# Six ring slots instead of eight, two weight chunks kept in SBUF, and the expert product one slot behind the dot

## The chip, the cores and the metric

The kernel runs on one core of a Trainium2 chip. The metric is device time in microseconds (us) of one execution, as the median of several. An execution with the hardware profiler on gives the trace; its own time stands beside its span below.

## What is computed

Two decoder layers over 256 tokens of width 1024, in float32. Layer 0 mixes tokens with differential attention, layer 1 with a short gated convolution; each is followed by a PEER expert layer: every token picks 8 x 16 = 128 of 16384 single-neuron experts and needs the rows u and v of each. The part that fills the time is this:

```python
q = (xt @ w_q).reshape(T, PEER_HEADS, 2, PEER_HALF)
s = jnp.einsum('thpd,hpkd->thpk', q, sub_keys).astype(F32)
s_top, i_top = lax.top_k(s, PEER_TOPK)
...
best, pos = lax.top_k(cand, PEER_TOPK)
idx = jnp.take_along_axis(cand_idx, pos, axis=-1)
gates = jax.nn.softmax(best, axis=-1)
...
    act = jnp.einsum('chkd,cd->chk', u_tab[ib], xb)
    act = (jax.nn.gelu(act.astype(F32)) * gb).astype(xb.dtype)
    return jnp.einsum('chk,chkd->cd', act, v_tab[ib])
```

## The kernel before

**Windows and slots.** There are four windows: the two blocks of 128 tokens, in layer 0 (windows 0 and 1) and in layer 1 (windows 2 and 3). A window has 128 slots, 512 in all. In a slot each of the 128 tokens (one per partition) uses one of its experts. POOL gathers the 128 rows (u beside v, 8 KB each, 1.05 MB together) into a slot of `ring` with an indirect DMA (L643). DVE multiplies u with the token's row and sums (`dot`, L1239). ACT makes the gelu, the weight and a diagonal matrix of the weights (`weigh`, L853, L855, L859). PE multiplies this diagonal with v into two PSUM banks that add up over the window (`add_expert`, L575: two calls, four matmul records in the trace) and raises `v_used`. At a window's end DVE adds the banks to the residual (`finish`, L1231), and the next window's first product waits for that (`acc_read`).

**The ring.** `ring` has 8 slots. The gather of slot s waits for `v_used` of slot s - 8 (L640), so a slot is busy from the issue of its gather until its expert product is done. The first eight gathers wait instead for products of the front (everything that runs before slot 0), since the ring's memory first holds weight chunks.

**Weight chunks.** The other operations of the next window (projections, attention or convolution, output, queries and ranking) are woven into the slots of the present one. A chunk of a weight matrix is 2 MB and is used by 8 matmul calls, one in each of 8 slots (L338, `project`). Chunks live at numbered places: 0 and 1 are the two halves of `wring` and are used in turn, 2 to 5 are pairs of ring slots and serve only the front, 6 is `spare`. SP issues the loads in one list (`loads`, L259 to L268). A load waits until the product on the chunk that held its place is written, and all loads behind it in the list wait with it. Chunk ("wq", 3) of windows 2 and 3 is one matrix part: it is loaded once, into place 6, and read in both windows.

**The order of work.** Every engine runs a loop over the slots and, at slot s, does its expert step and then every side step that is due at s. The due times are a table of numbers (`AT`, and the `LATE_` tables). On DVE and ACT the expert step at slot s is that of slot s. On PE it is that of slot s - 2 (L585 to L590). The side steps pass data between engines: PE makes a product, ACT copies it, PE transposes, DVE reads, each one or two slots later. An engine that waits for such a datum also holds up its later expert steps.

Of the kernel before, what the change touches and what calls it, by code (L numbers as in the profile page):

```python
# [14 lines left out]
P = 128  # L15
D = 1024
# [9 lines left out]
NKEYS = 128  # L26
EXPERTS = NKEYS * NKEYS
SLOTS = PH * TOPK
RING = 8
WINDOWS = DEPTH * (SEQ // P)  # L30
ALL = WINDOWS * SLOTS
CHUNK = 512
# [80 lines left out]
def along(sides, slot):  # L113

    for side in sides:
        while side["due"] is not None and side["due"] <= slot:
            side["due"] = next(side["steps"], None)
# [6 lines left out]
def build(nc, consts, x_rows, x_cols, bias_rows, ffn_rows, w_qkv, w_o, conv_w_in, conv_w_out, peer_w_q, peer_keys, peer_uv, out):  # L124
    with ExitStack() as ctx:
        def sb(name, shape, dt=F32):
            return ctx.enter_context(nc.sbuf_tensor(name, shape, dt))
# [4 lines left out]
        def sem(name):  # L132
            return ctx.enter_context(nc.semaphore(name))
# [15 lines left out]
        qk_gain, sub_gain, taps = of_const("qk_gain"), of_const("sub_gain"), of_const("taps")  # L149
        lam4 = of_const("lam").rearrange("p (i d) -> p i d", i=4)  # L150

        ring = sb("ring", [P, RING, 2 * D])
        wring = sb("wring", [P, 2, KT * CHUNK])
        rows = sb("rows", [P, 3 * D])
        rows1 = sb("rows1", [P, 2 * D])
# [41 lines left out]
        gains = sb("gains", [P, 2])  # L197
        dots = sb("dots", [P, RING])
        gelu = sb("gelu", [P, RING])
        weight = sb("weight", [P, RING])  # L200
        diag = sb("diag", [P, RING, P])

# [3 lines left out]
        def pool_of(name, banks=None):  # L206
            return Pool(banks or [psum(f"{name}0"), psum(f"{name}1")], [sem(f"{name}_written{i}") for i in range(2)],
                        [sem(f"{name}_read{i}") for i in range(2)])

        pp, tt, ss, ff = pool_of("pp"), pool_of("tt"), pool_of("ss"), pool_of("ff", acc)  # L210
# [29 lines left out]
        xf_made = sem("xf_made")  # L240
        uv_in = [sem(f"uv_in{i}") for i in range(RING)]
        dot_done = sem("dot_done")
# [18 lines left out]
        loads = [(0, *what) for what in first]  # L261
        later = [(1, "in", 2), (1, "in", 1), (0, "wq", 2), (1, "in", 3), (0, "wq", 3)]
        for n in range(1, WINDOWS):
            later += [(n, "in", c) for c in (2, 4, 3, 5, 0, 1)] if n > 1 else []
            later += [(n, "out", 0), (n, "out", 1), (n, "wq", 0), (n, "wq", 1), (n, "wq", 2), (n, "wq", 3)]
        later = [what for what in later if what not in ((2, "wq", 3), (3, "wq", 3))]
        loads += [(*what, (i + 1) % 2) for i, what in enumerate(later)]
        loads.insert([load[:3] for load in loads].index((2, "wq", 0)), (2, "wq", 3, 6))  # L268
        held_at = {}
        for place in range(7):  # L270
            for i, load in enumerate(load for load in loads if load[3] == place):
# [2 lines left out]
        def ring_at(s):  # L274
            return (s + 4) % RING

        def slot(s):

            return ring[:, ring_at(s), :], uv_in[ring_at(s)], 16 * (s // RING + 1)
# [17 lines left out]
        def weights(n, what, c):  # L297

            if (n, what) == (1, "in") and c in (0, 4, 5):
                n = 0  # L300
            if (n, what, c) == (3, "wq", 3):
                n = 2
            place, before = held_at[(n, what, c)]
            return places[place], w_in[place], 16 * (before + 1)

        def copied(eng, pool, *keys):

            for key in keys:
                eng.wait_ge(pool.read_sem(key), pool.times(key) + 1)

        def written(eng, pool, key):

            eng.wait_ge(pool.written_sem(key), pool.times(key) + 1)
# [5 lines left out]
        def _(pe):  # L319
# [93 lines left out]
            def front():  # L413
                low, high, every = range(4), range(4, KT), range(KT)
                pe.wait_ge(const_in, 16)
                pe.wait_ge(x_scaled, 1)
                pe.wait_ge(w_half_in, 16)
                first, _, _ = weights(0, "in", 0)
                by_row = first.rearrange("p (k n) -> p k n", k=KT)
                bank = take(pp, (0, "in", 0))  # L420
# [143 lines left out]
            def add_expert(s):  # L564

                n, k = divmod(s, SLOTS)
                if s == 0:
                    copied(pe, ff, (1, "in", 4), (1, "in", 5))
                if n and k == 0:
                    pe.wait_ge(acc_read, n)  # L570
                row, landed, count = slot(s)
                pe.wait_ge(landed, count)
                pe.wait_ge(diag_ready, s + 1)
                for half in range(2):
                    mm = nc.tensor.matmul(acc[half][:, :], diag[:, s % RING, :], row[:, D + half * 512:D + (half + 1) * 512],  # L575
                                          start=(k == 0), stop=(k == SLOTS - 1))
                mm.then_inc(v_used, 1)
# [5 lines left out]
            for n in (2, 3):  # L583
                sides += begun(gated_input(n), turn_gated(n), output(n), turn_output(n), *(experts(n, c) for c in range(4)))
            for s in range(ALL):  # L585
                if s > 1:
                    add_expert(s - 2)
                along(sides, s)
            add_expert(ALL - 2)
            add_expert(ALL - 1)  # L590


        @block.sync
        def _(sp):
            def load(n, what, c):
                place, landed, _ = weights(n, what, c)
                matrix = {"in": in_dram[n // 2], "out": out_w_dram[n // 2], "wq": peer_w_q[n // 2]}[what]
                if (n, what, c) == (0, "in", 0):
                    half = KT * CHUNK // 2
                    sp.dma_start(place[:, 0:half], matrix[c][:, 0:half]).then_inc(w_half_in, 16)  # L600
                    sp.dma_start(place[:, half:], matrix[c][:, half:]).then_inc(landed, 16)
                else:
                    sp.dma_start(place, matrix[c]).then_inc(landed, 16)

            sp.dma_start(xT[:, :, :].rearrange("p k t -> p (k t)"), x_cols[0]).then_inc(x_cols_in[0], 16)
            previous = {}
            for n, what, c, place in loads:
                if place in previous:
                    m, was, k = previous[place]
                    written(sp, pp, (m, "wqb" if (m, was, k) == (0, "wq", 0) else was, k))  # L610
                if place == 6:
                    sp.wait_ge(logit_max, 4)
                    written(sp, pp, (1, "values", 1))
                previous[place] = n, what, c
                load(n, what, c)
            for b in range(2):
                for c in range(2):
                    sp.wait_ge(h_finished, 2 * (2 + b) + c + 1)
                    sp.dma_start(out_dram[b][:, c * CHUNK:(c + 1) * CHUNK], h[:, b, c * CHUNK:(c + 1) * CHUNK]).then_inc(out_done, 16)
            sp.wait_ge(out_done, 64)  # L620


        @block.gpsimd
        def _(pool):
            for n in range(WINDOWS):
                for k in range(SLOTS):
                    s = n * SLOTS + k
                    if k % TOPK == 0:
                        pool.wait_ge(idx_ready, s // TOPK + 1)
                    if s < RING:  # L630
                        if ring_at(s) < 2:
                            written(pool, ff, (1, "in", 4))
                        elif ring_at(s) < 4:
                            written(pool, ff, (1, "in", 5))
                        elif ring_at(s) < 6:
                            written(pool, ff, (1, "in", 0))
                        else:
                            written(pool, pp, (0, "out", 0))
                    else:
                        pool.wait_ge(v_used, s - RING + 1)  # L640
                    dst, landed, _ = slot(s)
                    at = s % (2 * SLOTS)
                    nc.gpsimd.indirect_dma_start(dst, None, uv_dram, bass.IndirectOffsetOnAxis(idx[:, at:at + 1], 0)).then_inc(landed, 16)  # L643
# [229 lines left out]
        def _(dve):  # L873
            done = [0]

            def link(ins):

                done[0] += 1
                ins.then_inc(dve_step, 1)
                dve.wait_ge(dve_step, done[0])  # L880
# [343 lines left out]
            def finish(n):  # L1224

                b = n % 2
                yield SLOTS * (n + 1) + 1
                dve.wait_ge(v_used, SLOTS * (n + 1))
                for c in range(2):
                    hh = h[:, b, c * CHUNK:(c + 1) * CHUNK]  # L1230
                    link(nc.vector.tensor_tensor(hh, hh, acc[c][:, :], ALU.add))  # L1231
                    dve.sem_inc(h_finished, 1)
                dve.sem_inc(acc_read, 1)

            def dot(s):
# [5 lines left out]

            front()
            sides = begun(*(finish(n) for n in range(WINDOWS - 1)))
            sides += begun(second_head(), late_input(2), late(1), late_input(1), attention(0), late(2), late_input(3), late(3), attention(1),
                           output(1), *(experts(1, c) for c in range(4)))
            for n in (2, 3):
                sides += begun(gated_input(n), convolve(n), output(n), *(experts(n, c) for c in range(4)))
            for s in range(ALL):
                dot(s)
                along(sides, s)  # L1250
            whole(finish(3))


# [46 lines left out]
```

## Time and profile before

| | us |
|---|---|
| median of 3 runs (1577.06 to 1578.72) | 1578.14 |
| the profiled execution's own time | 1575.86 |
| its span in the trace | 1574.0 |
| front, until the first gather is issued | 101.6 |
| PE busy in matmuls | 1357.4 (86%) |
| DVE busy | 1005.6 (64%) |
| moved by DMA | 637.58 MB, mean 405 GB/s |
| of it the gathers | 536.90 MB |

PE, DVE, ACT and POOL are the engines; SP only issues loads. Times within the trace count from the span's start. The busy time of an overlapped matmul record is longer than its share of the engine: four records of an expert product follow each other in 1.72 us though the line says 1.88. A name with a q (DVEq) is the engine's sequencer. The idle time in brackets is that of the engine before the instruction, with what ended it.

### The profile page before, as it was taken

To read this page: it belongs to the slowest core of one execution; us is meant where nothing else is said; L and a number is where in the kernel's file an instruction comes from. 1 tells how busy PE (TensorE), PEld (TensorE's weight loads), DVE (VectorE), ACT (ScalarE), POOL (GpSimd) and SP (SyncE) were. 2 spreads that over 40 slices of the span, in tenths; PEclk is the share of its full clock that TensorE was granted. 3 is DMA by queue.
4 is the path that set the end of the run, shared out by engine and by line. 5 is a ranking of instruction groups with operands and counts; after the bars stand their busy time and mean duration, and the time that the engine had idled before them with its cause. 6 is when DMAs were issued, how large, how long until landed. Compare 5 with 4: busy or idle time off the path is not lost.

```text
span 1574.0 us, 13058 instructions
## 1 busy us (share of the span) xinstructions
PE 1357.4 (86%) x3288; PEld 587.2 (37%) x3288; DVE 1005.6 (64%) x2442; ACT 594.8 (38%) x1809; POOL 568.2 (36%) x516
## 2 busy tenths in 40 slices
PE   7899899888897988977989898879898887777777
PEld 3454344433343433333434343334343332222222
DVE  5686879964587864444467985444558896544454
ACT  1324354543342542332334443333334444333333
POOL 0024333543343433323444343323344453444341
PEclk9999999999998999989999899999899999999999
DMA  9469999999999999999999999999999999999996
GB/s 399 208 250 422 423 417 407 407 422 421 422 422 421 394 422 423 425 421 422 422 422 422 389 410 423 423 422 422 422 422 421 420 407 421 421 421 422 421 422 282
DMA packets 82297, 637.58 MB, mean 405 GB/s; under 512 B 9136, under 2 KB 9264, under 8 KB 10544
## 3 DMA queue, kind: packets, MB, share of 16 engines
q0 software_dynamic: 73728, 536.90, 82.4%
q1 hardware_dynamic: 7200, 93.85, 14.3%
q10 hardware_dynamic: 1296, 6.00, 0.9%
q8 instruction: 28, 0.46, 0.1%
q14 instruction: 45, 0.37, 0.1%
HBM read 635.67 MB, written 1.05 MB: 405 GB/s over the span
## 4 chain that ended last, share of the span: by engine, by line
DMA 39%; PE 36%; DVE 16%; ACT 4%; issue 4%; DVEq 0%; POOL 0%; SPq 0%; POOLq 0%; ACTq 0%
DMA ring<-in_peer_uv_dram,idx 38%; PE acc L575 22%; PE pp L338 10%; DVE ring L1239 7%; PE acc L338 1%; ACT diag L859 1%; PE tt L351 1%; DVE top_i L1025 1%; ACT weight L855 1%; DVE top L1021 1%; ACT L853 1%; ACT L722 1%; DVE row_f L1070 1%; ACT gelu L853 1%; PE pp L425 1%
## 5 line engine op out<-in xcount | busy, mean ns | idle before, releaser
L575 PE MATMUL acc<-ring,diag 128*128 128x512 f32 x2048 | 1003.9, 618 | 160.4 <-ACT diag L859 150.9
L1239 DVE CUSTOM_DVE_ANT_0 ring<-ring,xf 128x1024 f32<-128x1024 f32 x512 | 626.9, 1226 | 492.2 <-DMA ring<-in_peer_uv_dram,idx 480.5
L643 POOL DMA_INDIRECT ring<-in_peer_uv_dram,idx x512 | 568.0, 1109 | 982.9 <-PE acc L575 856.2
L575 PEld LDWEIGHTS acc<-ring,diag 128*128 128x128 f32 x2048 | 382.8, 196 | 705.3 <-issue 692.8
L853 ACT ACTIVATE gelu<-dots 128x1 f32<-128x1 f32 x512 | 103.5, 202 | 836.7 <-DVE dots L1239 836.4
L859 ACT ACTIVATE diag<-const,weight 128x128 f32<-128x128 f32 x512 | 205.5, 401 | 16.8
L855 ACT ACTIVATE weight<-gelu,gates 128x1 f32<-128x1 f32 x512 | 150.8, 295 | 16.6
L338 PE MATMUL pp<-wring,xT 128*128 128x512 f32 (+1 forms) x272 | 130.5, 578 | 1.2 <-ACT xT L662 1.2
L338 PE MATMUL pp<-wring,rows 128*128 128x512 f32 x192 | 99.6, 600 | 0.0
L338 PEld LDWEIGHTS pp<-wring,xT 128*128 128x128 f32 x272 | 52.0, 194 | 59.4 <-issue 56.5
L338 PE MATMUL pp<-wring,qTa 128*128 128x512 f32 x112 | 57.4, 601 | 0.0
L338 PEld LDWEIGHTS pp<-wring,rows 128*128 128x128 f32 x192 | 36.8, 193 | 45.8 <-issue 45.8
L1239 DVE DVE_READ_ACCUMULATOR2_ANT dots<- 128x1 f32 x512 | 41.9, 82 | 0.0
L410 PE MATMUL ss<-keysT,qT 128*128 128x128 f32 x128 | 21.0, 315 | 20.6 <-issue 20.6
L351 PE MATMUL tt<-const,rows 128*128 128x128 f32 x144 | 23.1, 285 | 17.0 <-DVEq L1199 11.3
L1025 DVE FIND_INDEX8 top_i<-top,score 128x8 uint32<-128x128 f32 x128 | 34.2, 285 | 0.0
L351 PEld LDWEIGHTS tt<-const,rows 128*128 128x128 f32 x144 | 17.7, 146 | 39.8 <-DVEq L1199 14.6
L338 PEld LDWEIGHTS pp<-wring,qTa 128*128 128x128 f32 x112 | 21.7, 195 | 27.2 <-issue 27.2
L410 PEld LDWEIGHTS ss<-keysT,qT 128*128 128x128 f32 x128 | 19.6, 224 | 30.6 <-issue 30.5
L1021 DVE MAX8 top<-score 128x8 f32<-128x128 f32 x128 | 28.1, 280 | 3.4 <-ACT score L718 2.4
L1025 DVE FIND_INDEX8 pos<-best,pick 128x8 uint32<-128x256 f32 x64 | 26.1, 418 | 0.0
L338 PE MATMUL pp<-wring,xf 128*128 128x512 f32 x48 | 25.0, 602 | 0.0
(114 smaller groups left out, 636.5 us busy)
## 6 DMA issues: line engine op xcount, KB each, us to landing
wring<-in_peer_w_q_dram SPq DMA_DIRECT2D x14, 2048.0 KB, 11.9
wring<-in_conv_w_in_dram SPq DMA_DIRECT2D x12, 2048.0 KB, 12.0
wring<-in_w_qkv_dram SPq DMA_DIRECT2D x5, 2048.0 KB, 12.0
ring<-in_peer_uv_dram,idx POOLq DMA_INDIRECT x512, 15.3
wring<-in_conv_w_out_dram SPq DMA_DIRECT2D x4, 2048.0 KB, 11.7
ring<-in_w_qkv_dram SPq DMA_DIRECT2D x3, 2048.0 KB, 32.0
wring<-in_w_o_dram SPq DMA_DIRECT2D x3, 2048.0 KB, 12.6
ring<-in_w_qkv_dram SPq DMA_DIRECT2D x2, 1024.0 KB, 8.6
```

The source lines that it names most:

```text
L338: mm = nc.tensor.matmul(bank[:, 0:width], src[:, k, :], by_row[:, k, columns], start=(k == 0), stop=(k == KT - 1))
L351: t = nc.tensor.transpose(bank[:, j * P:(j + 1) * P], tile, ident)
L410: mm = nc.tensor.matmul(bank[:, j * P:(j + 1) * P], qT[:, j, :], keysT[:, 4 * c + j, :], start=True, stop=True)
L425: mm = nc.tensor.matmul(bank[:, :], xT[:, k, :], by_row[:, k, :], start=(k == 0), stop=(k == KT - 1))
L575: mm = nc.tensor.matmul(acc[half][:, :], diag[:, s % RING, :], row[:, D + half * 512:D + (half + 1) * 512], start=(k == 0), stop=(k == SLO ...
L643: nc.gpsimd.indirect_dma_start(dst, None, uv_dram, bass.IndirectOffsetOnAxis(idx[:, at:at + 1], 0)).then_inc(landed, 16)
L853: nc.scalar.activation(gelu[:, r:r + 1], dots[:, r:r + 1], ACT.Gelu_apprx_tanh).then_inc(gelu_done, 1)
L855: nc.scalar.activation(weight[:, r:r + 1], gelu[:, r:r + 1], ACT.Copy, scale=gates[:, at:at + 1]).then_inc(weight_ready, 1)
L859: nc.scalar.activation(diag[:, r, :], ident, ACT.Copy, scale=weight[:, r:r + 1]).then_inc(diag_ready, 1)
L1021: ins = nc.vector.max(t, v)
L1025: ins = nc.vector.max_index(i, t, v)
L1239: nc.vector.tensor_tensor_reduce(row[:, 0:D], row[:, 0:D], xf[:, s // SLOTS % 2, :], 1.0, 0.0, ALU.mult, ALU.add, dots[:, s % RING:s % RIN ...
```

## The change

The ring's memory stays as large (8 rows), but the gathers use 6 of them. The last two rows, which are place 5, are now free for chunks for the whole run. The output chunk ("out", 0) of layer 0, which the front puts there for window 0, stays and is read again in window 1. Then ("wq", 2) of layer 1 is put there for window 2 and read again in window 3. The list of loads so has two loads less: the one of ("out", 0) for window 1 and the one of ("wq", 2) for window 3. Since chunks use places 0 and 1 in turn, chunks behind the omitted ones change places. On PE the expert product at slot s is that of slot s - 1, still ahead of the slot's side steps. DVE's `finish` comes one slot earlier. The first gathers' waits follow the new places of their slots.

```diff
-RING = 8
+ROWS = 8
+RING = 6
...
-        ring = sb("ring", [P, RING, 2 * D])
+        ring = sb("ring", [P, ROWS, 2 * D])
...
-        later = [what for what in later if what not in ((2, "wq", 3), (3, "wq", 3))]
+        kept = ((1, "out", 0), (2, "wq", 2), (2, "wq", 3), (3, "wq", 2), (3, "wq", 3))
+        later = [what for what in later if what not in kept]
         loads += [(*what, (i + 1) % 2) for i, what in enumerate(later)]
         loads.insert([load[:3] for load in loads].index((2, "wq", 0)), (2, "wq", 3, 6))
+        loads.insert([load[:3] for load in loads].index((2, "wq", 0)), (2, "wq", 2, 5))
...
             for s in range(ALL):
-                if s > 1:
-                    add_expert(s - 2)
+                if s:
+                    add_expert(s - 1)
                 along(sides, s)
-            add_expert(ALL - 2)
             add_expert(ALL - 1)
...
                     m, was, k = previous[place]
+                    if (n, what, c) == (2, "wq", 2):
+                        m = 1
...
-                        elif ring_at(s) < 6:
+                        else:
                             written(pool, ff, (1, "in", 0))
-                        else:
-                            written(pool, pp, (0, "out", 0))
...
-                yield SLOTS * (n + 1) + 1
+                yield SLOTS * (n + 1)
                 dve.wait_ge(v_used, SLOTS * (n + 1))
```

PE at slot 24 of window 0. `pp<-wring` is a side product of one slot, `ss<-kT,qTa` are the first attention logits of window 1, `acc<-ring,diag` is an expert product, and `uv_in` names the ring slot that it reads. Before:

```order
L575 MATMUL acc0<-ring,diag 128x512 [waits diag_ready,uv_in2]
L575 MATMUL acc1<-ring,diag 128x512
L338 MATMUL pp0<-wring,xf 128x512
L368 MATMUL ss1<-kT,qTa 128x256 [waits ss_read1,tt_read0,tt_read1]
L368 MATMUL ss1<-kT,qTa 128x256
L368 MATMUL ss0<-kT,qTa 128x256 [waits ss_read0]
```

The same place of the changed kernel:

```order
L580 MATMUL acc0<-ring,diag 128x512 [waits diag_ready,uv_in3]
L580 MATMUL acc1<-ring,diag 128x512
L343 MATMUL pp0<-wring,xf 128x512
L373 MATMUL ss1<-kT,qTa 128x256 [waits ss_read1,tt_read0,tt_read1]
L373 MATMUL ss1<-kT,qTa 128x256
L373 MATMUL ss0<-kT,qTa 128x256 [waits ss_read0]
```

The ring slots read differ: before, the product ahead of the logits is that of slot 22 (22 + 4 is 26, ring slot 2 of 8); now it is that of slot 23 (27, ring slot 3 of 6). One more expert product stands ahead of the logits.

DVE at the border from window 0 to window 1. `ring,dots<-ring,xf` is the dot of a slot and `h<-h,acc` is `finish`. Before:

```order
L1239 ISA ring,dots<-ring,xf 128x1024 [waits uv_in4,dve_step]
L1239 ISA dots 128x1
L1057 TENSOR_SCALAR pos2<-pos 128x2x16
L1058 TENSOR_SCALAR pos2<-pos 128x2x16 [waits dve_step]
L1059 CAST pos_f<-pos2 128x64 [waits dve_step]
L1239 ISA ring,dots<-ring,xf 128x1024 [waits uv_in5,dve_step]
L1239 ISA dots 128x1
L1231 TENSOR_TENSOR h<-h,acc0 128x512 [waits v_used]
L1231 TENSOR_TENSOR h<-h,acc1 128x512 [waits dve_step]
```

The same place of the changed kernel:

```order
L1243 ISA ring,dots<-ring,xf 128x1024 [waits uv_in0,dve_step]
L1243 ISA dots 128x1
L1235 TENSOR_TENSOR h<-h,acc0 128x512 [waits v_used]
L1235 TENSOR_TENSOR h<-h,acc1 128x512 [waits dve_step]
L1061 TENSOR_SCALAR pos2<-pos 128x2x16 [waits dve_step]
L1062 TENSOR_SCALAR pos2<-pos 128x2x16 [waits dve_step]
L1063 CAST pos_f<-pos2 128x64 [waits dve_step]
L1243 ISA ring,dots<-ring,xf 128x1024 [waits uv_in1,dve_step]
```

`finish` moved from behind the dot of slot 129 to behind the dot of slot 128.

## Rows read from the trace of the kernel before

**Rows 1.** The page: DMA busy share and rate in 40 equal slices.
```profile
DMA  9469999999999999999999999999999999999996
GB/s 399 208 250 422 423 417 407 407 422 421 422 422 421 394 422 423 425 421 422 422 422 422 389 410 423 423 422 422 422 422 421 420 407 421 421 421 422 421 422 282
```

**Rows 2.** Windows, busy time by engine; last columns: PE's clock, DMA share, GB/s.
```profile
226.00:331.00 105.00, 92.25 (x268) 44.23 (x267) 95.50 (x262) 53.15 (x152) 45.09 (x38) 0.95 1.00 409
...
490.00:535.00 45.00, 38.93 (x98) 17.61 (x97) 41.93 (x122) 18.91 (x57) 16.34 (x13) 0.92 0.97 396
...
878.00:923.00 45.00, 41.67 (x108) 19.02 (x107) 42.20 (x133) 24.36 (x68) 19.77 (x15) 0.96 0.97 384
```

**Rows 3.** The page: issues of one kind of load, count, size, median time to landing.
```profile
wring<-in_peer_w_q_dram SPq DMA_DIRECT2D x14, 2048.0 KB, 11.9
```

**Rows 4.** The source view of the gathers' line, all 512.
```profile
DMA to landing us min/median/max: 5.5/15.3/24.7
```

**Rows 5.** Timeline of all engines near the end: start, duration, instruction, idle time before.
```profile
1548.20 1.96 PE L575 MATMUL acc<-ring,diag 128*128 128x512 f32 x4 [0.55 <-ACT diag L859]
...
1550.43 0.94 POOL L643 DMA_INDIRECT ring<-in_peer_uv_dram,idx  x1 [1.56 <-PE acc L575]
...
1550.78 1.23 DVE L1239 CUSTOM_DVE_ANT_0 ring<-ring,xf 128x1024 f32<-128x1024 f32 x1 [1.26 <-DMA ring<-in_peer_uv_dram,idx]
...
1553.16 1.95 PE L575 MATMUL acc<-ring,diag 128*128 128x512 f32 x4 [0.54 <-ACT diag L859]
1553.27 1.22 DVE L1239 CUSTOM_DVE_ANT_0 ring<-ring,xf 128x1024 f32<-128x1024 f32 x1 [1.25 <-DMA ring<-in_peer_uv_dram,idx]
```

**Rows 6.** Timeline around slot 24: expert product 22, first logits, DVE's bias.
```profile
183.54 1.96 PE L575 MATMUL acc<-ring,diag 128*128 128x512 f32 x4 [0.83 <-ACT diag L859]
...
186.28 1.14 PE L368 MATMUL ss<-kT,qTa 64*128 64x256 f32 x8
...
187.45 0.69 DVE L957 TENSOR_TENSOR rows<-ss,spare 128x512 f32<-128x512 f32 x1 [2.13 <-PE ss L368]
```

**Rows 7.** Timeline, slots 31 to 38: expert product 31, scores of slot 36, DVE's ranking.
```profile
213.23 3.65 PE L575 MATMUL acc<-ring,diag 128*128 128x512 f32 x4 [3.30 <-ACT diag L859]
...
224.88 1.05 PE L410 MATMUL ss<-keysT,qT 128*128 128x128 f32 x8
...
226.66 0.87 DVE L1021 MAX8 top<-score 128x8 f32<-128x128 f32 x4 [1.77 <-ACT score L718]
```

**Rows 8.** Timeline, slot 51: DVE's bias waits for the logits of slot 50.
```profile
270.80 0.69 DVE L957 TENSOR_TENSOR rows<-ss,spare 128x512 f32<-128x512 f32 x1 [0.59 <-PE ss L368]
```

**Rows 9.** Timeline: expert product 71, expert product 84, dot 90.
```profile
326.89 1.96 PE L575 MATMUL acc<-ring,diag 128*128 128x512 f32 x4 [1.50 <-ACT diag L859]
...
360.88 1.88 PE L575 MATMUL acc<-ring,diag 128*128 128x512 f32 x4
...
371.08 1.23 DVE L1239 CUSTOM_DVE_ANT_0 ring<-ring,xf 128x1024 f32<-128x1024 f32 x1 [1.25 <-DMA ring<-in_peer_uv_dram,idx]
```

**Rows 10.** Timeline of SP: loads issued once slots 80 and 347 let them.
```profile
347.76 0.33 SPq L603 DMA_DIRECT2D wring<-in_peer_w_q_dram  x1
...
1148.83 0.33 SPq L603 DMA_DIRECT2D wring<-in_peer_w_q_dram  x1
```

**Rows 11.** Timeline of PE after two window borders: expert products 128, 134, 259.
```profile
493.65 3.40 PE L575 MATMUL acc<-ring,diag 128*128 128x512 f32 x4 [2.99 <-DVEq L1233]
...
516.68 1.96 PE L575 MATMUL acc<-ring,diag 128*128 128x512 f32 x4 [0.71 <-ACT diag L859]
...
895.69 1.88 PE L575 MATMUL acc<-ring,diag 128*128 128x512 f32 x4
```

**Rows 12.** Timeline of POOL: the gathers of slots 140 and 265.
```profile
511.63 0.94 POOL L643 DMA_INDIRECT ring<-in_peer_uv_dram,idx  x1 [4.76 <-PE acc L575]
...
891.82 0.94 POOL L643 DMA_INDIRECT ring<-in_peer_uv_dram,idx  x1 [1.03 <-PE acc L575]
```

**Rows 13.** DMA view of 891.5 to 892.5 us: the gather of slot 265 to its landing.
```profile
ring<-in_peer_uv_dram,idx POOLq DMA_INDIRECT x1, 8.6
```

More of the change, by code:

```diff
@@ L300, in weights @@
                 n = 0
-            if (n, what, c) == (3, "wq", 3):
+            if (n, what) == (3, "wq") and c > 1:
                 n = 2
+            if (n, what, c) == (1, "out", 0):
+                n = 0
             place, before = held_at[(n, what, c)]
```

## The prediction, on record before the changed kernel ran

> **What bounds the kernel now.** I read the page's slices first, then the windows, then the timeline at places where a wait ends last. From the fourth slice on the DMA line shows 9 everywhere and the rate is about 422 GB/s [rows 1]: once the gathers run, the 16 DMA engines are full. Only three stretches sag, to 409, 396 and 384 GB/s [rows 2]: slots 39 to 68 of window 0, and the two borders after slots 128 and 256. Near the end the machine shows its bare rhythm [rows 5]. Dots start 2.49 us apart (1550.78, 1553.27), each released by its gather, and 1.05 MB at 422 GB/s is 2.48 us. A slot's dot at 1550.78 leads to its expert product's end at 1555.11, so a slot is free 4.3 us after its landing. The product that ends at 1550.16 lets the next gather go at 1550.43, 0.27 us later. The quickest gather of all took 5.5 us from issue to landing [rows 4]. So DMA is the bound, and PE, DVE and ACT count only where they free ring slots too late.
>
> **Bytes removed.** One 2048 KB load [rows 3] is 2.10 MB, at 422 GB/s 4.97 us. Two go: 9.9 us at most. What matters is where the hole opens. Because places 0 and 1 are used in turn, the load for window 1 that disappears from its old time is not the one of slot 40 (the next chunk takes its turn) but the one released by slot 80, at 347.76; the other is the one released by slot 347, at 1148.83 [rows 10]. A third load, released by slot 247, moves to slot 183, behind two others. It moves bytes within a stretch that is DMA-bound throughout, so I count 0; if the triple left PE behind afterwards, it would show at the border of slot 256, below.
>
> **What a shorter ring asks.** With six slots the next landing in the same slot can't come sooner than slot freed + 0.27 + 5.5 us. DMA runs full without a load in flight if that is within 6 x 2.49 = 14.9 us of the landing: the slot must be free 9.2 us after it landed. With eight it was 14.1 us. The tail needs 4.3 us [rows 5], so the last 120 slots lose nothing. Where the trace gives no such case (no gather there starved), both ends come from rows: 0 us, and two gathers of buffer, 4.97 us, for each place.
>
> The Trainium skill, DMA: Bandwidth & Descriptors, section "Anatomy of one DMA — SWDGE (gpsimd) path", fits a lone DMA as 2.0 us plus bytes over 436 GB/s, an estimate of 4.4 us for this gather. The trace disagrees, with 5.5 us as the least of 512 [rows 4]. By the page each of the three starved places below would cost 1.1 us less, and the sum would be lower by 3.3 us.
>
> **The expert product one slot earlier.** Two effects. Where PE runs without a gap, one side product fewer (two calls of 0.43 us each, 0.86 us) stands ahead of a slot's release: a gain of 0.86 us. But each side step of PE now stands behind one expert product more (1.72 us), and where the product had been waiting for ACT's diagonal, behind the side product of the slot as well (0.86 us), which before ran in the gap. Whoever waits for the side step waits longer. In windows 2 and 3 these data are a slot early and I price it at 0, cover being the 2.49 us of a slot. In window 0 DVE waits for them, and it is never idle for long from 187 to 331 us: busy 95.5 of 105 us after 226 [rows 2]. Step by step:
> - Slot 24: product 22 starts at 183.54 after a wait of 0.83; the logits end at 187.4 and DVE's bias, which waited 2.13, follows at 187.45 [rows 6]. Now product 22 at 183.54, the side product of slot 23, product 23, side product and logits: 183.54 + 1.72 + 0.86 + 1.72 + 0.86 + 1.1 = 189.8. DVE is 2.4 us late.
> - Slot 36: product 31 waits for a diagonal that hangs on this DVE work, 213.23 [rows 7]; it moves by 2.4. Between it and the scores stand one product and one side product more (2.58 us, of which small transposes hide 0.1). The ranking that started at 226.66 starts at 231.6: 4.9 late.
> - Slot 51: DVE waited 0.59 for logits [rows 8]. They stand behind one more product: with 4.9 us already lost, 1.5 more, 6.4.
> - Slots 61 to 66: the ring of six lets dots 61 and 62 land some 0.4 us behind DVE's delayed time, and the mixed values come 0.3 us late: 7.1 us in all.
> Product 71 again starts on a diagonal [rows 9], so the whole run of PE behind it, without a gap to slot 90, is 7.1 us late less 0.86. Product 84 ended at 362.76; now 369.0. The gather of slot 90 may then land at 369.0 + 0.27 + 5.5 = 374.8, against 371.08 [rows 9]: 3.7 us late, although the 4.97 us load of 347.76 is gone. With the next load behind, DMA is full again and the rest stays. Term: **+3.5 us** (the first saving is lost and more). Without the delay it would be -3.6; so the term lies between -3.6 and +3.5, with the next places apart.
>
> **The borders.** After slot 128 PE waited 2.99 us for `finish` [rows 11]. With `finish` one slot earlier, DVE waits for product 127 instead, a few tenths behind dot 128, and product 128 starts some 2.5 us earlier. Queued behind DVE's wait are a ranking step and dot 129, which before waited for its gather anyway. DVE, full from there on, gains 1 us by it. Against that: the gather of slot 140 left at 511.63 [rows 12]. With six slots it waits for product 134, which ended at 518.6 [rows 11] and would end at 517.4: 6 us later. A 2 MB load issued at 516 fills most of the hole, since it gets the engines alone. I take **+1.5 us**, between 0 and 4.97. After slot 256 the gather of slot 265 left at 891.82 and landed at 900.4 [rows 12, 13]. Now product 259 (895.69 + 1.88 = 897.6) must be done, so it lands at 903.3: 2.9 late, less up to 3.0 for the earlier `finish`, which DVE's own backlog gives back by slot 262. I take **+1.7 us**, between 0 and 4.97. After slot 384 the same gain meets a smaller need: 0. The load of 1148.83 lies in a full stretch with slots free in 5 to 8 us: **-5.0 us** in full. The start: gathers 2 to 5 leave up to 6 us later, but PE's first expert products, from 116 us on, set the pace and DVE has slack there: 0, at most +0.8.
>
> **Sum.** +3.5 + 1.5 + 1.7 - 5.0 = +1.7 us on 1575.86, the profiled execution's own time, is 1577.6. That execution is 2.3 us under the median of 1578.14, so the forecast for the median is 1579.8. A measurement here tells about 0.2%, 3.2 us, from no change; the forecast is "the same".
>
> **Rivals.**
> 1. *The delay in window 0 is not real or is absorbed.* For it: DVE does have gaps of 4.4 us at slot 37. Against: the chain runs through product 31 and the scores, not through dot 37 [rows 7]. Then the first term is -3.6 and the sum -5.4: 1572.7. Chance 0.21.
> 2. *Bytes alone decide*, -9.9 us: 1568.2. For it: the full DMA line [rows 1]. Against: the sag where ring slots are freed late [rows 2]. Chance 0.09. The Trainium skill, Perfetto Trace Analysis, section "Engine Utilization" (Roofline), calls a kernel below the ridge memory-bound, which read plainly gives this rival; the sagging rows speak against it.
> 3. *The ring of six starves (slower).* Place: the two borders, where DVE has four slots' backlog. Price: both give up their whole two gathers of buffer, 2 x 4.97 instead of 3.2, and the least latency under load is nearer 6.3 us than 5.5, 0.8 at three places. Sum +3.5 + 9.9 + 2.4 - 5.0 = +10.8: 1589. It decides from slots that are freed more than 9.2 us after landing. Half of it already makes the kernel slower by over 0.2%. Chance 0.28.
> 4. *The change doesn't do what it says.* The list of loads is two shorter in the built program. Chance 0.01 or less.
>
> **Chances.** Forecast 0.41, rival 1 0.21, rival 2 0.09, rival 3 0.28, rest 0.01. Faster by over 0.2%: 0.31. Within: 0.41. Slower: 0.28. The range 1571 to 1587 leaves out rival 2 and the far half of rival 3.
>
> **What would show it.** Right: 633.4 MB moved; the tail at 2.49 us per slot; the ranking of slot 38 near 231 us and dot 90 near 375; rates under 400 GB/s after slots 128 and 256; product 128 starting without a 3 us wait. Wrong: dot 90 before 369 (rival 1), or a rate of 422 GB/s through both borders (rival 2), or gathers there issued with none in flight for more than 5 us in sum (rival 3). What would overturn the frame: dots more than 2.5 us apart in the tail, since then six slots don't feed the DMA at all, at up to 0.1 us for each of 120 slots for every 0.6 us by which the latency exceeds 10.3 us.

## The result: slower by 1.6%, and the profile after

| | before | changed |
|---|---|---|
| median of 6 runs each, us | 1576.69 | 1601.42 |
| ratio, 95% interval | | 1.0159, 1.0141 to 1.0177 |
| span in the trace, us | 1574.0 | 1597.5 |
| moved by DMA, MB | 637.58 | 633.39 |

The change costs 25 us. The forecast was +1.7 us and the range ended at 1587, so it was wrong. The kernel before appears here with six executions instead of the first three. The bytes are those foreseen, 4.19 MB fewer. The page of the changed kernel, DMA busy share and rate in 40 slices (of 40 us each), and the bytes:

```profile
DMA  9469989899999899999999999999999999999997
GB/s 401 197 246 405 378 357 381 352 401 402 422 421 419 343 424 422 423 424 421 417 421 412 392 377 422 423 422 417 422 420 422 408 405 416 422 421 422 421 422 320
DMA packets 82009, 633.39 MB, mean 396 GB/s; under 512 B 9104, under 2 KB 9232, under 8 KB 10512
```

Against [rows 1], slices 4 to 10 (120 to 399 us, window 0) no longer stand at 407 to 423 GB/s but at 352 to 405, and slice 14 (the border after slot 128) at 343 instead of 394. Slice 24, behind the border after slot 256, has 377 instead of 410. From slice 25 to slice 39 the two rows differ by at most 12. Most of the loss is in window 0. The windows view of the changed kernel, by stretch (last columns: PE's clock, DMA share, GB/s):

```profile
106.00:129.00 23.00, 20.65 (x49) 8.93 (x48) 18.25 (x52) 7.83 (x21) 9.30 (x9) 1.00 0.95 340
182.00:196.00 14.00, 13.41 (x39) 5.87 (x38) 7.58 (x17) 8.42 (x21) 5.80 (x5) 0.97 0.82 290
219.00:227.00 8.00, 7.55 (x13) 3.36 (x14) 3.79 (x8) 4.72 (x15) 1.56 (x2) 0.70 0.29 96
267.00:282.00 15.00, 12.47 (x40) 5.72 (x39) 12.26 (x33) 8.15 (x20) 3.88 (x4) 1.00 0.81 293
304.00:320.00 16.00, 16.00 (x39) 7.21 (x38) 12.58 (x34) 5.62 (x19) 6.56 (x7) 0.84 0.73 265
345.00:392.00 47.00, 45.21 (x109) 20.19 (x109) 23.86 (x40) 19.38 (x63) 20.38 (x18) 1.00 0.99 387
526.00:543.00 17.00, 14.84 (x33) 6.50 (x34) 16.11 (x51) 11.82 (x34) 5.64 (x5) 0.90 0.67 241
916.00:935.00 19.00, 17.75 (x57) 8.83 (x56) 18.16 (x49) 10.33 (x35) 9.05 (x7) 1.00 0.90 329
```

The first five stretches of the kernel before, for comparison:

```profile
106.00:129.00 23.00, 21.51 (x51) 9.34 (x50) 19.57 (x56) 10.32 (x27) 10.02 (x10) 1.00 1.00 403
182.00:196.00 14.00, 13.17 (x41) 5.73 (x40) 10.99 (x28) 6.67 (x21) 5.15 (x4) 1.00 1.02 426
219.00:227.00 8.00, 8.00 (x29) 4.19 (x28) 2.80 (x6) 3.21 (x10) 2.81 (x3) 1.00 0.98 408
267.00:282.00 15.00, 15.00 (x53) 7.54 (x51) 13.56 (x30) 8.99 (x25) 7.88 (x7) 1.00 1.01 420
304.00:320.00 16.00, 13.12 (x43) 6.43 (x42) 15.03 (x37) 4.79 (x16) 7.83 (x7) 0.97 1.01 425
```

The worst stretch, 219 to 227 us, moved 96 GB/s where the kernel before had 408.

**How the lateness grows.** The start of a slot's dot in the changed kernel, minus the start of the same dot before, minus the same difference at slot 0 (the front varies by up to 2.5 us from one execution to the next), names the places. This table is read from the dot starts of each trace, in us; E1 to E10 are the experiments below. Two more, E5 and E9, are within 2.2 us of zero at every slot of this table (in between, single slots are up to 4.8 us early or late).

| slot | changed | E1 | E2 | E3 | E4 | E6 | E7 | E8 | E10 |
|---|---|---|---|---|---|---|---|---|---|
| 9 | 3.6 | 0.3 | 2.0 | 3.0 | 3.1 | 0.2 | 2.0 | -0.4 | 3.1 |
| 27 | 6.1 | 2.9 | 2.4 | 3.0 | 7.4 | 0.2 | 4.5 | -0.4 | 3.0 |
| 39 | 11.7 | 5.8 | 5.2 | 5.7 | 12.9 | 0.1 | 8.0 | -0.5 | 4.3 |
| 54 | 15.7 | 8.2 | 8.1 | 8.2 | 16.8 | 0.2 | 10.3 | -0.4 | 8.9 |
| 66 | 20.3 | 8.3 | 13.8 | 13.1 | 21.7 | 0.1 | 12.2 | -0.4 | 13.7 |
| 84 | 23.3 | 8.4 | 22.0 | 16.0 | 26.8 | 0.3 | 12.6 | -0.4 | 17.3 |
| 93 | 20.2 | 8.2 | 18.3 | 12.3 | 24.5 | -0.1 | 12.3 | -0.5 | 12.0 |
| 120 | 20.4 | 8.3 | 20.0 | 12.5 | 25.1 | 0.0 | 12.5 | -0.3 | 12.7 |
| 141 | 24.6 | 7.4 | 22.4 | 15.4 | 30.6 | 4.9 | 16.7 | 0.3 | 18.2 |
| 192 | 29.4 | 8.6 | 24.3 | 24.3 | 30.7 | 11.3 | 15.4 | 1.4 | 22.8 |
| 240 | 29.3 | 7.8 | 27.3 | 24.6 | 30.6 | 10.2 | 14.7 | 5.9 | 22.8 |
| 264 | 26.1 | 8.5 | 27.8 | 20.9 | 31.8 | 6.8 | 15.4 | 2.8 | 19.0 |
| 276 | 31.5 | 8.3 | 35.2 | 28.3 | 37.2 | 12.2 | 16.0 | 8.2 | 24.3 |
| 288 | 28.6 | 7.3 | 32.0 | 24.9 | 34.5 | 9.2 | 15.5 | 5.3 | 21.4 |
| 348 | 28.9 | 7.4 | 33.2 | 26.9 | 35.5 | 9.2 | 14.9 | 5.4 | 21.5 |
| 360 | 23.9 | 7.3 | 33.1 | 22.7 | 35.4 | 5.0 | 14.9 | 0.4 | 16.5 |
| 511 | 23.3 | 6.7 | 34.1 | 25.6 | 35.7 | 5.3 | 14.1 | 0.5 | 16.9 |

The changed kernel is 20.4 us late when window 0 ends. It falls back by 4.2 more at the border of slot 128 and by 4.9 more where the third load now stands at slot 183 (most of it is made good just before slot 256). It makes good 5.0 where the second load is missing, between slots 348 and 360.

**One place in full.** Around slots 31 to 38 of the changed kernel. POOL's gathers 37 and 38, PE's product 31, DVE's dots 37 and 38 and the first step of the ranking, from the timeline:

```profile
219.45 3.75 PE L580 MATMUL acc<-ring,diag 128*128 128x512 f32 x4 [4.82 <-ACT diag L863]
...
223.47 0.94 POOL L647 DMA_INDIRECT ring<-in_peer_uv_dram,idx  x1 [8.29 <-PE acc L580]
226.38 0.94 POOL L647 DMA_INDIRECT ring<-in_peer_uv_dram,idx  x1 [1.97 <-PE acc L580]
...
230.08 1.23 DVE L1243 CUSTOM_DVE_ANT_0 ring<-ring,xf 128x1024 f32<-128x1024 f32 x1 [7.11 <-DMA ring<-in_peer_uv_dram,idx]
...
236.24 1.23 DVE L1243 CUSTOM_DVE_ANT_0 ring<-ring,xf 128x1024 f32<-128x1024 f32 x1 [4.92 <-DMA ring<-in_peer_uv_dram,idx]
...
237.39 0.87 DVE L1025 MAX8 top<-score 128x8 f32<-128x128 f32 x4
```

Product 31 waits for a diagonal, as before [rows 7], 6.2 us later. With eight slots its end released the gather of slot 39; with six it releases that of slot 37. No other gather is in flight when gather 37 is issued (the one before landed at 220.55), and DVE stands 7.1 and 4.9 us for dots 37 and 38. Gather 37 took 6.6 us to land. Gather 38 took 9.8, with a 2 MB load beside it that SP issued at 224.4. The scores end on PE at 235.1 (their row starts at 234.10), but the ranking begins behind dot 38, at 237.39.

### The profile page after: what moved, and what is told of

Its sections match the earlier page's. It is cut to its first block, busy times and chain, and to the rows that moved or that the text cites. A ratio compares the mean times of both kernels' runs of the same rounds, so it can differ in the third digit from the quotient of the medians.

```text
span 1597.5 us, 13058 instructions
## 1 busy us (share of the span) xinstructions
PE 1359.0 (85%) x3288; PEld 580.9 (36%) x3288; DVE 1005.6 (63%) x2442; ACT 595.6 (37%) x1809; POOL 563.2 (35%) x516
## 2 busy tenths in 40 slices
DMA packets 82009, 633.39 MB, mean 396 GB/s; under 512 B 9104, under 2 KB 9232, under 8 KB 10512
## 3 DMA queue, kind: packets, MB, share of 16 engines
HBM read 631.48 MB, written 1.05 MB: 396 GB/s over the span
## 4 chain that ended last, share of the span: by engine, by line
DMA 37%; PE 36%; DVE 16%; ACT 6%; issue 4%; POOL 0%; DVEq 0%; SPq 0%; POOLq 0%; ACTq 0%
DMA ring<-in_peer_uv_dram,idx 36%; PE acc L580 23%; PE pp L343 10%; DVE ring L1243 8%; ACT diag L863 1%; PE acc L343 1%; ACT weight L859 1%; ACT L857 1%; ACT gelu L857 1%; DVE top_i L1029 1%; DVE row_f L1074 1%; ACT L726 1%; DVE top L1025 1%; DVE pick L1071 1%; DVE pick L1068 1%
## 5 line engine op out<-in xcount | busy, mean ns | idle before, releaser
L580 PEld LDWEIGHTS acc<-ring,diag 128*128 128x128 f32 x2048 | 377.5, 195 | 777.5 <-issue 766.8
L863 ACT ACTIVATE diag<-const,weight 128x128 f32<-128x128 f32 x512 | 205.4, 401 | 16.7
L343 PE MATMUL pp<-wring,xT 128*128 128x512 f32 (+1 forms) x240 | 112.7, 568 | 1.2 <-ACT xT L666 1.2
L343 PEld LDWEIGHTS pp<-wring,xT 128*128 128x128 f32 x240 | 45.8, 194 | 52.4 <-issue 49.5
L343 PE MATMUL pp<-wring,qTa 128*128 128x512 f32 x96 | 50.0, 612 | 0.0
L343 PE MATMUL pp<-ring,xT 128*128 128x512 f32 x80 | 37.8, 592 | 0.0
L343 PEld LDWEIGHTS pp<-wring,qTa 128*128 128x128 f32 x96 | 18.7, 196 | 23.3 <-issue 23.3
L356 PE MATMUL tt<-const,rows 128*128 128x128 f32 x144 | 21.7, 273 | 3.4 <-DVEq L1002 3.4
## 6 DMA issues: line engine op xcount, KB each, us to landing
wring<-in_peer_w_q_dram SPq DMA_DIRECT2D x12, 2048.0 KB, 11.7
wring<-in_conv_w_in_dram SPq DMA_DIRECT2D x12, 2048.0 KB, 11.7
ring<-in_peer_uv_dram,idx POOLq DMA_INDIRECT x512, 10.3
wring<-in_conv_w_out_dram SPq DMA_DIRECT2D x4, 2048.0 KB, 11.7
ring<-in_w_qkv_dram SPq DMA_DIRECT2D x3, 2048.0 KB, 31.8
```

What stands on the lines that cost most here:

```text
L343: mm = nc.tensor.matmul(bank[:, 0:width], src[:, k, :], by_row[:, k, columns], start=(k == 0), stop=(k == KT - 1))
L356: t = nc.tensor.transpose(bank[:, j * P:(j + 1) * P], tile, ident)
L863: nc.scalar.activation(diag[:, r, :], ident, ACT.Copy, scale=weight[:, r:r + 1]).then_inc(diag_ready, 1)
```

## The experiments

The lag is the number of slots by which PE's expert product stands behind the dot: two before, one (the shorter lag) in the change. A handshake is a wait of one engine for data of another. Theory R: the ring of six is the cost, in window 0. Theory L: PE's side steps behind one product more are the cost.

**E1, the shorter lag alone.**

```diff
-                if s > 1:
-                    add_expert(s - 2)
+                if s:
+                    add_expert(s - 1)
...
-                yield SLOTS * (n + 1) + 1
+                yield SLOTS * (n + 1)
```

> Ring of eight and the list of loads as before; only PE's product one slot behind the dot, and finish one slot earlier. Theory R (the ring of six is the cost: slots freed 12 to 17 us after landing in window 0 starve it): with eight slots the late side steps cost little, +2 to +4 us in window 0, and the earlier finish gives 1 to 2 back at the borders, so within 0.2% of before, about 1579; the steps of +2.5 at slot 24 and +1.5 at slot 51 are seen in the trace. Theory L (side steps of PE behind one product more are the cost, and DVE's chain of window 0 is the bound): +10 us or more, near 1590.

Measured 1585.0 us, ratio 1.005 (1.0031 to 1.0069), +8 us (8.7 between the medians): between the two. The timeline at slot 24, PE's products 22 and 23, the logits, and DVE's bias:

```profile
186.24 1.96 PE L575 MATMUL acc<-ring,diag 128*128 128x512 f32 x4 [0.57 <-ACT diag L858]
188.03 1.02 PE L338 MATMUL pp<-wring,xf 128*128 128x512 f32 x2
188.88 1.88 PE L575 MATMUL acc<-ring,diag 128*128 128x512 f32 x4
190.60 1.02 PE L338 MATMUL pp<-wring,xf 128*128 128x512 f32 x2
191.55 1.14 PE L368 MATMUL ss<-kT,qTa 64*128 64x256 f32 x8
...
192.72 0.69 DVE L956 TENSOR_TENSOR rows<-ss,spare 128x512 f32<-128x512 f32 x1 [4.70 <-PE ss L368]
```

DVE waits 4.70 us where it waited 2.13 [rows 6]: +2.6, forecast 2.4. In the table it is 2.9 late at slot 27, 5.8 at 39 and 8.2 at 54, and nothing after that. The chain of waits of the prediction (2.4, 4.9, 6.4, 7.1) is real and was 1 us short. With eight slots most of it is kept to the end (6.7).

**E2, the ring of six alone** (six slots, all loads, the longer lag).

```diff
-RING = 8
+ROWS = 8
+RING = 6
```

> Gathers use six ring slots; the list of loads, PE's product two slots behind and finish as before. Theory R: window 0 starves at the same places as in the changed kernel, and every slot is freed up to 2.6 us later than there, so it is slower than it: +30 to +40 us on before, 1607 to 1617, since two loads of 5 us also come back. Theory L: the shorter ring alone costs the +1.5 and +1.7 of the borders and a few us at the front, +7, near 1584.

Measured 1613.04 us, 1.0233 (1.0211 to 1.0255), +37 us. Theory R. By the table 13.8 us are lost by slot 66 with no side step moved, and 22.0 by slot 84.

**E3, the changed kernel with the longer lag.** The edit is the reverse of E1's, in the changed kernel.

> The changed kernel with PE's product two slots behind the dot and finish in its old place. Theory R: the shorter lag is a help to a short ring and costs only where DVE waits for logits, so without it the kernel is equal or slower than the changed one: 1600 to 1610. Theory L: without the late side steps most of the loss goes: 1580 or less.

Measured 1604.34 us, 1.0179 (1.0154 to 1.0205): as slow as the changed kernel. The longer lag wins 8 us up to slot 93 (12.3 against 20.2); at slot 348 only 2 of them are left (26.9 against 28.9), and at the end it is behind (25.6 against 23.3). With six slots the later release of ring slots costs as much as the handshakes save.

**E4, the changed kernel without the kept chunks.**

```diff
-        kept = ((1, "out", 0), (2, "wq", 2), (2, "wq", 3), (3, "wq", 2), (3, "wq", 3))
-        later = [what for what in later if what not in kept]
+        later = [what for what in later if what not in ((2, "wq", 3), (3, "wq", 3))]
...
-        loads.insert([load[:3] for load in loads].index((2, "wq", 0)), (2, "wq", 2, 5))
```

> The changed kernel with the list of loads as before (the two more chunks are loaded again); ring of six and lag of one. Both theories: the kept chunks give back what the trace of the changed kernel shows at slots 85 to 88 and 356, 4.7 and 5.0 us, so without them 9.7 us more than the changed kernel, 1609 to 1611. If the missing bytes bring nothing in window 0, because PE and not DMA sets the pace there, 5 us more: 1605.

Measured 1612.73 us, 1.0227 (1.0209 to 1.0246): 11 us over the changed kernel, with an uncertainty of about 4. The kept chunks bring about what their bytes are worth, 9.9 us. The two ring slots that they take away cost 37 us with the longer lag (E2), and with the shorter one 28 on top of E1's 8.7 (E4).

**E5, the shorter lag from slot 126 on**, ring of eight. E6 and E8 use the same edit.

```diff
+                for past in range(max(s - (2 if s <= 126 else 1), 0), s + 1 - (2 if s < 126 else 1)):
+                    add_expert(past)
```

> Ring of eight and loads as before; PE's product two slots behind up to slot 125 and one behind from slot 126 on, finish one slot earlier. Theory P (places: the shorter lag costs only where DVE waits for a side step, in window 0): the 8.7 us of the kernel with the shorter lag everywhere are gone and its later trace, which gained 1.5 us from slot 54 to the end, is all that is left: 1574 to 1576. Rival (the shorter lag costs through all windows): it keeps a part of the 8.7, 1580 or more.

Measured 1576.24 us, 0.9999 (0.9987 to 1.0011). From slot 126 on, the shorter lag and the earlier `finish` are worth nothing measurable with eight slots.

**E6, everything but window 0.** Rows of the ring are given out by a table: each slot takes the row that has been idle longest among the first `size`.

```diff
+            size = 8 if s < 130 else 6
+            r = min((used[r], r) for r in used if r < size)[1]
```

> Window 0 as before (eight ring slots, product two slots behind, the output chunk loaded again); from slot 126 on the product is one slot behind, from slot 130 on the ring has six slots, and the query chunk of layer 1 is kept as in the changed kernel. Theory P: window 0 alone cost 20 us; the changed kernel's trace loses 3.0 us more from slot 126 on, so 1579 to 1581. Rival (the delay of window 0 hid later starvation, since later loads and slots ran with more slack behind a late DVE): the later windows show losses of their own, 1587 or more.

Measured 1584.01 us, 1.0053 (1.003 to 1.0077), +8 us: window 0 was most of the loss, but the rest was expected 3 to 5 us lower. The trace shows 5.3 us at the end, where the changed kernel's later windows lose 2.9. The excess comes in small pieces: the border of slot 128 costs 4.9 us (4.2 in the changed kernel), the moved load 5.7 (5.6 late at slot 180, 11.3 at 192; 4.9 in the changed kernel).

**E7, a ring of seven**, all loads, the shorter lag: `size = 7`.

> The kernel with the shorter lag everywhere and loads as before, with a ring of seven: between a ring of eight (1585.0) and one of six (1612.7). Theory P with a point of starvation (a slot must be free 9.2 us after landing with six, 11.6 with seven, 14.1 with eight): the slots of window 0 that are freed 12 to 17 us after landing still starve it, those at 9 to 12 no longer: a third of the 27.7 us, 1592 to 1596. Rival (each slot taken away costs the same): 1599.

Measured 1593.74 us, 1.011 (1.0085 to 1.0135), inside the 1592 to 1596 of the starvation theory. From eight to seven slots costs 9 us, from seven to six (E4) 19. So a ring slot has no fixed price; the result fits a price that grows with the number of slots that are freed too late. That forecast used the prediction's limit, 11.6 us for seven slots, so it doesn't tell which limit is right.

**E8, six slots only while the chunk of layer 1 lies there** (slots 218 to 381), the version that could have beaten the kernel before. The output chunk is loaded again.

```diff
+            size = 6 if 218 <= s < 382 else 8
```

> Six ring slots only while the query chunk of layer 1 lies in the other two, from slot 218 to 381; else eight; the output chunk is loaded again; product one slot behind from slot 126 on. Theory P: -5.0 us for the load that goes, +4.1 for the border of slot 256 with six slots, -1 for the shorter lag: 1573 to 1576, about as before. Rival (the border costs nothing once window 0 is not late): 1570.

Measured 1576.62 us, 0.9998 (0.9986 to 1.001). The 5.0 us come back between slots 348 and 360 (5.4 to 0.4), and were lost before, between slots 192 and 288 (1.4 to 5.3), a stretch with the border of slot 256. No version here beats the kernel before.

**E9 and E10, the lag by place**: two slots behind in slots 20 to 69, one elsewhere, with eight slots and all loads (E9), and in the changed kernel (E10).

```diff
+                lag = 2 if 20 <= s < 70 else 1
+                for past in range(added, s + 1 - lag):
+                    add_expert(past)
+                added = max(added, s + 1 - lag)
```

> The kernel with ring of eight, loads as before and product one slot behind, but with the product two slots behind in slots 20 to 69. Theory D (the 8.7 us of the shorter lag are DVE's waits for the logits of slot 24, the scores of slot 36, the logits of slot 50 and the values after it): all of it goes, 1575 to 1579. Rival (the cost comes from PE's order as such, at any place): most of it stays, 1582 or more.

> The changed kernel, with the product two slots behind in slots 20 to 69 and one behind elsewhere. If the traces add up by place: the kernel with six slots, kept chunks and the longer lag stands 13 us behind at slot 66 and the changed one 20, and from there to the end the changed one loses 3 us and the other 12.5; so the better half of each gives +16, 1591 to 1595. Rival (the starvation of window 0 eats what the longer lag gives): 1598 to 1602.

E9 measured 1577.17 us, 1.0003 (0.9992 to 1.0014): all of E1's 8 us is gone, so they arose in those 50 slots, where E1's trace shows DVE waiting for a side step. E10 measured 1595.03 us, 1.013 (1.0112 to 1.0149), at the upper end of the forecast range: about 5 us better than the changed kernel, where the traces give 6.4 (23.3 to 16.9). The two costs add up by place.

**E11, what a short ring can sustain**, measured where nothing else runs: the kernel before, with six, five and four slots in the tail.

```diff
+            size = 8 if s < 400 else 6 if s < 436 else 5 if s < 474 else 4
```

> The kernel before, with a ring of eight up to slot 399, of six in slots 400 to 435, of five in 436 to 473, of four from 474 on. These slots have no side work and are free 4.4 us after landing, 4.7 to the next issue. Theory F (one gather in flight is enough; a ring of N keeps the rate if 4.7 + 5.5 us are under N x 2.49): dots 2.49 us apart with six and with five, 2.55 with four, so +2 us in all. Rival (the rate needs more gathers in flight): dots more than 2.49 apart already with six or five, and near 3 with four, +20 us.

A single execution took 1599.78 us. The windows view inside the stretches of six, five and four slots:

```profile
1320.00:1370.00 50.00, 38.15 (x79) 13.44 (x79) 24.62 (x42) 19.11 (x61) 20.80 (x21) 1.00 1.01 419
1400.00:1470.00 70.00, 53.10 (x110) 18.44 (x109) 33.64 (x56) 24.25 (x81) 27.30 (x27) 1.00 1.00 408
1500.00:1570.00 70.00, 48.53 (x92) 17.32 (x92) 28.42 (x46) 20.66 (x69) 24.11 (x22) 0.93 0.90 337
```

Six slots carry nearly the full rate (419 GB/s; the kernel before has 421 in the same stretch). The tail of the changed kernel agrees: 2.49 us per slot from slot 400 to 508, as forecast. Five give dots 2.58 us apart (slots 444 to 472), four 3.10 (480 to 508), against 2.49 and 2.48 of the kernel before in the same slots. From a gather's issue to its dot it took 8.2 us on average with five slots and 7.5 with four, not 5.5. The cycle closes: a slot was freed 4.6 us after its dot, 0.3 later the next gather was issued, and 4.6 + 0.3 + 7.5 = 12.4 = 4 x 3.10. The 4.6 were 4.3 with five slots; PE's clock, granted at 1.00 there and at 0.93 on average with four, may be part of that 0.3.

**E12, late slots instead of few.** Tail with six slots, where each product is held back by one or two slots.

```diff
-                pe.wait_ge(diag_ready, s + 1)
+                held = 0 if s < 410 else 1 if s < 461 else 2
+                pe.wait_ge(diag_ready, min(s + 1 + held, ALL))
```

> The kernel before, with a ring of six from slot 400 on, where PE's product of slot s also waits for the diagonal of slot s + 1 (slots 410 to 460) or s + 2 (from 461 on), so that a slot is free 4.4 us plus one or two slots after its landing: 6.9 and 9.4. The prediction's rule (free within 9.2 us is enough; a gather needs 5.5 us): 2.49 us per slot in the first part, 2.54 in the second, 2 us in all. The rule read from the tail with five and four slots (a gather needs near 8 us, whatever frees the slot late): 2.57 in the first, 3.07 in the second, 4 + 29 us, near 1608.

A single execution took 1613.7 us. The windows view, one slot held and two:

```profile
1350.00:1440.00 90.00, 69.36 (x143) 23.83 (x141) 43.51 (x72) 32.16 (x108) 34.88 (x35) 1.00 1.01 413
1480.00:1580.00 100.00, 69.07 (x131) 24.16 (x130) 39.85 (x66) 29.64 (x99) 35.66 (x33) 0.93 0.93 344
```

Dots are 2.56 us (slots 412 to 460) and 3.07 us (466 to 508) apart, where the prediction's rule gave 2.49 and 2.54 and the rule read from E11 2.57 and 3.07. In this tail, what counts is the time that is left to a gather between the freeing of its slot and the moment at which the data is due.

## Why the prediction was wrong

Two steps of the prediction failed, both in the term for window 0: it priced one place and left the others out, and it took too short a time for a gather.

- **Window 0 was priced at one place.** The term +3.5 came from the gather of slot 90 alone. The places ahead of it were put at 0 (the start) and 0.4 us (dots 61 and 62), with PE's pace and DVE's slack as cover. The prediction's own limit, a slot free 9.2 us after landing, already spoke against this. In window 0 of the trace before, 74 of the 128 slots are freed later than that (with eight slots 14.1 us were allowed), and 40 still are in the changed kernel. Measured: 3.6 us at the start (forecast 0, at most 0.8), 20.3 by slot 66, 23.3 by slot 84, 20.2 at slot 93 (forecast 3.7 for dot 90). At some of these places DVE already waited for gathers before the change. Its timeline before, dots 12 and 37, which the prediction's rows leave out:

```profile
144.15 1.23 DVE L1239 CUSTOM_DVE_ANT_0 ring<-ring,xf 128x1024 f32<-128x1024 f32 x1 [4.93 <-DMA ring<-in_peer_uv_dram,idx]
...
221.18 1.23 DVE L1239 CUSTOM_DVE_ANT_0 ring<-ring,xf 128x1024 f32<-128x1024 f32 x1 [4.42 <-DMA ring<-in_peer_uv_dram,idx]
```

An engine's wait for a gather is no slack for a later gather: at the start gather 9 lands 3.7 us later than before, and its dot starts 3.7 us later.

- **What a shorter ring asks.** The prediction took the quickest gather of 512, 5.5 us, for the time that a gather needs at full rate. E11 and E12 show about 8.2 us for 96% of the rate, which leaves a slot 14.9 - 0.3 - 8.2 = 6.4 us with six slots. In the changed kernel's window 0, 84 slots are freed later than that. Window 0 agrees with the tail where no load is in flight, as the gathers of slots 75 to 80 and of slots 81 to 88 show (source view of the gathers' line in the changed kernel, 343 to 358 us and 358.5 to 377.5 us):

```profile
DMA to landing us min/median/max: 5.6/7.3/8.0
...
DMA to landing us min/median/max: 7.8/8.1/8.4
```

The first six were issued with two others in flight and landed 3.05 us apart on average. The other eight were issued with three in flight and landed 2.48 us apart: the full rate, at some 8 us each. The Trainium skill, DMA: Bandwidth & Descriptors, section "Anatomy of one DMA — SWDGE (gpsimd) path", gave 4.4 us, further away still; its fit is for one DMA.

How the miss divides between the two steps was not separated. A rough estimate from the trace before: give each gather of window 0 the end of product s - 6 plus 0.27 us plus a fixed time, and let each shortfall against its dot push back all that follows. With the prediction's 5.5 us this gives 15 us by slot 84, with the 6.3 of rival 3 it gives 33, and E2 measured 22. So even with a time close to the one taken, the places left out show most of the loss. With 8.2 us the same sum is 100, far too much: that figure holds for steady rotation and is not the price of every late slot.

- **The handshakes** were right. DVE's delays by the shorter lag were forecast as 7.1 us (0.3 of it for the ring) and are 8.2 in E1; E9 places them in slots 20 to 69.
- **The two causes together**: I had asked whether the delay of the side steps was real or absorbed. It adds up with the other: at slot 66 the ring alone is 13.8 us late (E2), the lag alone 8.3 (E1), and both 21.7 with all loads (E4), 20.3 in the changed kernel. Behind slot 66, where PE has no gap, the shorter lag gives 2 to 3 us back (18.3 + 8.2 against 24.5 at slot 93, 20.0 + 8.3 against 25.1 at 120), more than the 0.86 that I had counted.
- **The borders**: forecast +1.5 and +1.7, measured 4.2 after slot 128, and 4.2 after slot 256 (29.3 to 28.6, with 4.9 of the moved load come back). E4, where no load is moved, has 5.5 and 3.9; E1, with eight slots, -0.9 and -0.5. Both are near the far end, the 4.97 us each that rival 3 took. `finish` did start product 128 some 3.6 us earlier (510.40 against 493.65, 20.4 us late), yet PE still waited 4.09 us for it, where I had said it would not. The reading that only three stretches sag also passes over a fourth, the slice at 407 GB/s after slot 384 [rows 1]; no term hangs on it.
- **The loads**: -5.0 at the second place (28.9 to 23.9), as forecast. The first, in window 0, gave 3.1 net (23.3 to 20.2). The moved load, put at 0, cost 4.9 at slot 183 for a time.
- **The rivals.** Rival 3 had the mechanism and the sign, at a chance of 0.28, but put it at the borders only: 1589. Its own test, gathers issued at the borders with none in flight for more than 5 us in sum, would have missed it. After slot 0 the changed kernel has three such gathers in all (37, 61 and 138), with 2.9, 0.5 and 1.5 us of nothing in flight. The rate falls already with two in flight. The range ended where the near bound of that price ended; a sum over all slots of window 0 was never worked out.

What stays open: why a gather takes 7.5 us in steady rotation with four slots, and 8.2 with five, but 5.5 to 6.6 when it is issued with none in flight (four in the changed kernel, slot 0 among them). Dividing by the time between dots, 2.4 gathers are in flight on average with four slots and 3.2 with five; only the sum of their times was measured. How much each of the two failed steps cost is open too. E6's excess of some 3 us was located and not explained.

## What to carry over

Before you trade a buffer for bytes, go through every slot and count those that are freed too late, not only the place that looks worst. A ring's slot must be free early enough for the time that a transfer takes at the rate you need, not for its quickest. Measure that time where nothing else runs, by taking slots away in steps. A place where an engine already waits for the transfer has no cover: a later transfer makes it wait longer. And a shorter lag helps the buffer and hurts whoever waits for the side steps, so choose it by place.

## What the chip showed that I had not expected

Rings of four slots with gathers of 1.05 MB moved 337 GB/s, of five 408, of six 419, each in one execution; by the 5.5 us of the quickest gather five should have been enough, and four nearly. Taking slots away and freeing them late came to the same: six slots, each held two slots longer, moved 344 GB/s, about as much as four (337).
